# RWKV pairs: the layer norm of a pair's y is spread over the next pair's levels and scan, and the next pair's first products follow the last chunk directly

## The chip, the cores and the metric

The kernel runs on one core of a Trainium2 chip. The metric is the device time of one execution in microseconds (us), lower is better. Engines: PE (TensorE, matrix products), PEld (its weight loads), DVE (VectorE), ACT (ScalarE), POOL (GpSimd), SP (SyncE, which issues most loads).

## The reference, cut to what matters

The program is one block of mixed attention (NSA beside RWKV-7), followed by a second block; the change touches the RWKV part alone, which for S = 512 tokens and 8 heads of 64 computes

```
w = -softplus(-(w0 + tanh(wd) @ w_up)) - 0.5;  decay = exp(-exp(w))
a = sigmoid(a0 + ad @ a_up);  g = sigmoid(gd) @ g_up
kk = k * k_k, normed over each head;  kh = k * (1 + (a - 1) * k_a)
# scan over tokens, per head, state 64 x 64:
state = state * decay + (state @ -kk) (kk * a)^T + v kh^T;  y = state @ r
y = (y - mean) * rsqrt(var + eps) * ln_w + ln_b       # over each head
y = (y + sum(r * kh * r_k) * v) * g
```

## The kernel before, in words

All tensors lie with channels on the 128 partitions and the 512 tokens along the free axis, so a tile of 128 x 512 holds two heads, a *pair*. There are PAIRS = 4 pairs, one after the other. The scan over tokens is done in NCH = 8 chunks of 64.

A pair p goes through four parts:
- **The head** (function `head` on each engine): `w`, `a`, `g` are the low-rank products on PE, `sw`, `a`, `g` their copies on ACT. `kk0` scales the key, `kkq` squares it, `kss` sums over a head (PE, four products), `kstd` is the square root (ACT), `kmax`, `krec`, `krexp` (DVE) clip, invert and expand it, `krs` transposes it, `kkn` applies it. `cs`, `rel`, `dsum`, `relm` are the cumulative decays (DVE), `Ep`, `En`, `Em`, `D` their exponentials (ACT). `a1`, `kh`, `A`, `B`, `rk` (DVE) and `kka`, `K`, `R` (POOL) form the scaled operands, `bonus` the last term of y. `tokA`, `tokB`, `tokK`, `tokV` turn operands to token-major (PE, then ACT copies), `P1` and `P2` are the score products, taken out through a mask by DVE into TR and MR.
- **The levels**: a triangular inverse is built by doubling in five levels. In each, PE forms A (L2061), DVE takes it through a mask into Ap (`L1a`, `L1b`, ..., L1436), PE multiplies on both sides (X in L2070, Y in L2072) and ACT copies X and XT back. `XT0` (L1425) starts it, on an XT refilled with the identity (`eye`, L1408).
- **The scan**: after `MV`, `U0`, `WT`, each chunk c goes PE `u` (L2105), DVE `U` (L1449), PE `s` (L2115), DVE `S` (L1453), with `SD` (L1447) beside it. The output y gathers in PSUM bank 7 (L2091, L2098, L2119).
- **The norm of y**: ACT copies y (L863), PE takes the `mean`, DVE centres it (`yc`), ACT squares it (`ysq`), PE sums (`vss`), ACT takes the root (`vstd`, with its table of functions), DVE inverts and expands (`vrec`, `vrexp`), PE transposes (`vrs`), DVE forms `yn`, `yb`, `o`.

Each engine runs its instructions in the order of its program, and that order is written out by hand: the lists RW_PE_REST, RW_ACT_REST, RW_DVE_REST name the steps of pair p, and a step with "+" in front belongs to the head of pair p + 1, which is worked off between the levels of pair p. Each step raises its engine's semaphore by one, and the other engines wait for `upto(list, (name, pair))`. The names `given`, `done`, `took`, `made`, `own` in the code are such waits for PE, ACT, ACT, DVE and the own engine. All steps of a DVE head wait for the step before them on DVE itself. The eight PSUM banks are shared out by hand too: 0 and 1 serve the head and the norm, 2 and 3 the A products, 4 and 5 Y, 6 and 7 X.

Of the kernel before, what the change touches and what calls it, by code (L numbers as in the profile page):

```python
# [64 lines left out]
for _name, _n in [("ident", 128), ("means", 128), ("pair", 128), ("perm", 128)]:  # L65
# [5 lines left out]
RW_PE_HEAD = ["w", "a", "kss", "krs", "g", "bonus", "tokA", "tokB", "tokV", "P1a", "P1b", "tokK"]  # L71
RW_PE_REST = (["P2a", "+w", "+a", "P2b", "X0a", "X0b", "XSa", "XSb", "A1a", "A1b", "+kss", "X1a", "Y1a", "X1b", "Y1b",
               "A2a", "A2b", "+krs", "X2a", "Y2a", "X2b", "Y2b", "A3a", "A3b", "X3a", "Y3a", "X3b", "Y3b",
               "A4a", "A4b", "+g", "X4a", "Y4a", "X4b", "Y4b", "A5a", "A5b", "+bonus", "Y5a", "Y5b", "MV", "U0", "WT"]
              + [x for c in range(NCH) for x in ((f"u{c}", f"s{c}") if c < NCH - 1 else (f"u{c}",))]
              + ["y", "+tokA", "mean", "+tokB", "+tokV", "+P1a", "+P1b", "vss", "+tokK", "vrs"])
RW_ACT_HEAD = ["sw", "a", "kkq", "kstd", "Ep", "En", "Em", "D", "g", "tokA", "tokB", "tokV", "tokK"]
RW_ACT_REST = ["+sw", "+a", "+kkq", "X0a", "X0b", "X1a", "T1a", "X1b", "T1b", "+kstd", "X2a", "T2a", "X2b", "T2b",
               "+Ep", "+En", "X3a", "T3a", "X3b", "T3b", "+Em", "+D", "X4a", "T4a", "X4b", "T4b", "+g", "T5a", "T5b",
               "MV", "U0", "y", "+tokA", "+tokB", "+tokV", "ysq", "vstd", "+tokK"]  # L80
RW_DVE_HEAD = ["kk0", "cs", "rel", "dsum", "relm", "kmax", "krec", "krexp", "kkn", "a1", "kh", "A", "B",
               "rk", "bonus", "eye", "P1a", "P1b"]
RW_DVE_REST = (["XT0", "+kk0", "P2a", "P2b", "+cs", "+rel", "+dsum", "L1a", "L1b",
                "+relm", "+kmax", "+krec", "+krexp", "L2a", "L2b", "+kkn", "+a1", "+kh", "L3a", "L3b",
                "+A", "+B", "L4a", "L4b", "+rk", "L5a", "L5b", "+bonus", "WT"]
               + [x for c in range(NCH) for x in ((f"SD{c}", f"U{c}", f"S{c}") if c < NCH - 1 else (f"U{c}",))]
               + ["+eye", "yc", "+P1a", "+P1b", "vrec", "vrexp", "yn", "yb", "o"])


RW_POOL_HEAD = ["kka", "K", "R"]  # L90
RW_POOL_REST = ["+kka", "+K", "+R"]


def pair_steps(head, rest):

    steps = [(x, 0) for x in head]
    for p in range(PAIRS):
        steps += [(x[1:], p + 1) if x[0] == "+" else (x, p) for x in rest if x[0] != "+" or p + 1 < PAIRS]
    return steps


RW_PE, RW_ACT, RW_DVE = (pair_steps(RW_PE_HEAD, RW_PE_REST), pair_steps(RW_ACT_HEAD, RW_ACT_REST),
                         pair_steps(RW_DVE_HEAD, RW_DVE_REST))
# [44 lines left out]
def build(nc, A, out, first_block=True, second_block=True):  # L148
# [3 lines left out]
    with ExitStack() as ctx:  # L152
# [130 lines left out]
        if first_block:  # L283
# [3 lines left out]
            def mixer_phase(*tensors):  # L287
# [20 lines left out]
             eye, mask8) = mixer_phase(  # L308
# [6 lines left out]
                ("kst", [P, TT, 2], F32), ("krec", [P, TT, 2], F32), ("eye", [P, HD], F32),  # L315
# [8 lines left out]
            rmask = norm_t[:, 1]  # L324
            stri = mask8[:, 0:2 * HD]
# [159 lines left out]
        def _(pool):  # L485
# [90 lines left out]
        def _(act):  # L576
# [104 lines left out]
            if first_block:  # L681
# [118 lines left out]
                def head(p, *names):  # L800
# [4 lines left out]
                    for name in names:  # L805
# [31 lines left out]

                head(0, *RW_ACT_HEAD)

                AHEAD = {1: ("kstd",), 2: ("Ep", "En"), 3: ("Em", "D"), 4: ("g",), 5: ()}  # L840
                for p in range(PAIRS):
                    head(p + 1, "sw", "a", "kkq")

# [4 lines left out]
                    for n in range(2):  # L848
                        taken("X0" + "ab"[n], X, 6, n)
                    for lev in range(1, 6):  # L850
# [4 lines left out]
                        head(p + 1, *AHEAD[lev])  # L855
                    given(p, "MV")
                    rw(p, "MV", act.activation(MV, psum[:, 0, :], ACT.Copy))
                    given(p, "U0")
                    rw(p, "U0", act.activation(U0[:].rearrange("p c d -> p (c d)"), psum[:, 1, :],
                                               ACT.Copy))  # L860
                    given(p, "y")
                    act.wait_ge(rw_pool, upto(RW_POOL, ("K", min(p + 1, PAIRS - 1))))
                    rw(p, "y", act.activation(tA[:], psum[:, 7, :], ACT.Copy))  # L863
                    head(p + 1, "tokA", "tokB", "tokV")
                    done(p, "yc")
                    rw(p, "ysq", act.activation(tB[:], tC[:], ACT.Square))
                    given(p, "vss")
                    rw(p, "vstd", act.activation(kst[:].rearrange("p t c -> p (t c)"), psum[:, 1, 0:8], ACT.Sqrt,
                                                 bias=eps[:, 1:2], scale=1.0 / HD))
                    head(p + 1, "tokK")  # L870
# [121 lines left out]
        def _(dve):  # L992
# [167 lines left out]
            if first_block:  # L1160
# [184 lines left out]
                def head(p, *names):  # L1345
# [11 lines left out]
                    for name in names:  # L1357
                        if name == "kk0":
                            if p >= 2:
                                own(p - 2, "o")  # L1360
                            step("kk0", dve.tensor_scalar(tC[:], k, v("k_k", p), None, ALU.mult))
# [11 lines left out]
                        if name == "relm":  # L1373
                            given(p, "kss")
# [29 lines left out]
                        if name == "bonus":  # L1404
                            given(p, "bonus")
                            step("bonus", dve.tensor_tensor(tD, val, psum[:, 1, :], ALU.mult))
                        if name == "eye":
                            rw(p, "eye", dve.tensor_copy(XT[:], eye[:].unsqueeze(1).to_broadcast([P, 8, HD])))  # L1408
                        if name[0:2] == "P1":
                            keep_lower(p, name, TR, {"a": 3, "b": 4}[name[2]])  # L1410

                head(0, *RW_DVE_HEAD)

                AHEAD = {1: ("relm", "kmax", "krec", "krexp"), 2: ("kkn", "a1", "kh"), 3: ("A", "kka", "B", "K"),
                         4: ("R", "rk"), 5: ("bonus",)}
                for p in range(PAIRS):
                    D_p = Dc[:, p % 2]

                    def step(name, ins, wait=True):
                        rw(p, name, ins)  # L1420
                        if wait:
                            own(p, name)

                    own(p, "P1b")
                    step("XT0", dve.copy_predicated(XT[:], lmask[:, 0].unsqueeze(1).to_broadcast([P, 8, HD]), TR[:, :, 0]),  # L1425
                         wait=False)
                    head(p + 1, "kk0")
                    for name, b in (("P2a", 5), ("P2b", 2)):
                        keep_lower(p, name, MR, b)
                    head(p + 1, "cs", "rel", "dsum")  # L1430

                    for lev in range(1, 6):
                        mask = lmask[:, lev].unsqueeze(1).to_broadcast([P, 4, HD])
                        for n in range(2):
# [3 lines left out]
                                psum[:, 2 + n, 0:4 * HD].rearrange("p (m n) -> p m n", m=4)), wait=False)  # L1438
                        head(p + 1, *AHEAD[lev])
                    given(p, "WT")  # L1440
                    step("WT", dve.tensor_copy(WT[:], psum[:, 2, :]), wait=False)
                    done(p, "U0")
                    for c in range(NCH):
                        if c < NCH - 1:
                            if c >= 1:
                                own(p, f"S{c - 1}")
                            step(f"SD{c}", dve.tensor_scalar(SD[:], Sh[:, c], D_p[:, c:c + 1], None, ALU.mult), wait=False)  # L1447
                        given(p, f"u{c}")
                        step(f"U{c}", dve.tensor_tensor(Ut[:, c], U0[:, c], psum[:, 3, 0:HD], ALU.add), wait=False)  # L1449
                        if c < NCH - 1:  # L1450
# [950 lines left out]
```

## Time and profile before

| | us |
|---|---|
| median of 3 runs (lowest, highest) | 3045.91 (3044.82, 3048.0) |
| profiled execution | 3043.87 |
| its span, first to last instruction | 3042.2 |
| RWKV pairs within the span | from about 387 to 616 |
| PE busy over the span | 2893.9 (95%) |
| DVE, ACT, POOL busy | 1469.2, 973.6, 196.8 |
| mean granted clock of TensorE | 0.957 of 2.4 GHz |

The profile is of one execution. Times in its views count from the span's first instruction. In the timeline an instruction group "xN" is N instructions in a row, and a bracket tells how long its engine sat idle before it and who ended that; in the chain of waits each piece is what held up the end at that time, so that the pieces of a stretch add up to it.

### The profile page before, as it was taken

How to read it: one execution, taken by the hardware profiler on the slowest of the kernel's cores; microseconds unless marked ns; L12 is line 12 of the kernel's file. 1: busy time of each engine (PE TensorE's matmuls, PEld its weight loads, DVE VectorE, ACT ScalarE, POOL GpSimd, SP SyncE). 2: the span in 40 equal slices, each digit the busy share in tenths (PEclk: the TensorE clock that was granted, in tenths of full speed). 3: DMA queues.
4: the chain of work that ended last, by engine and by line, in shares of the span. 5: the costliest groups of instructions: out<-in, count | busy, mean ns of one | idle time of the engine just before them, and what ended most of it. 6: DMA issues, size and time to landing. Idle time of an engine off the chain costs nothing.

```text
span 3042.2 us, 39851 instructions
## 1 busy us (share of the span) xinstructions
PE 2893.9 (95%) x15739; PEld 2296.4 (75%) x15739; DVE 1469.2 (48%) x2135; ACT 973.6 (32%) x1540; POOL 196.8 (6%) x241
## 2 busy tenths in 40 slices
PE   7988978899999999999979999999999989999998
PEld 6844857778788787888858888788887753788887
DVE  4255655366677655555453332333323468433322
ACT  3334234333333223222233222322223236332222
POOL 1000010001200011000110000100001000100000
PEclk8669988999999999999979999999999999899999
DMA  6100500057322364555412223222232210122232
GB/s 225 59 1 1 187 16 2 3 187 235 131 96 97 100 201 157 193 192 190 154 53 90 96 94 92 84 104 97 94 94 96 83 63 1 56 87 96 94 93 72
DMA packets 89905, 309.17 MB, mean 102 GB/s; under 512 B 10288, under 2 KB 14000, under 8 KB 89648
## 3 DMA queue, kind: packets, MB, share of 16 engines
q1 hardware_dynamic: 69040, 231.84, 22.7%
q0 software_dynamic: 20736, 75.51, 7.4%
q8 instruction: 94, 1.54, 0.2%
q14 instruction: 35, 0.29, 0.0%
HBM read 305.21 MB, written 2.10 MB: 101 GB/s over the span
## 4 chain that ended last, share of the span: by engine, by line
PE 88%; DVE 7%; ACT 2%; issue 1%; DMA 0%; POOL 0%; SPq 0%; DVEq 0%; ACTq 0%
PE psum L1688 24%; PE psum L1690 24%; PE psum L1689 24%; PE psum L1912 1%; PE psum L1900 1%; PE psum L1852 1%; PE psum L1762 1%; PE psum L1702 1%; PE psum L1758 1%; DVE nmax L1623 1%; PE psum L1759 1%; PE psum L2017 1%; PE psum L2072 1%; PE psum L2237 1%; PE psum L1924 1%
## 5 line engine op out<-in xcount | busy, mean ns | idle before, releaser
L1000 DVE TENSOR_TENSOR w_lo<-stage,w_hi 128x1024 fp32r<-128x1024 f32 (+3 forms) x445 | 519.4, 1167 | 846.9 <-ACT w_hi L586 844.7
L1688 PE MATMUL psum<-h_hi,w_hi 128*128 128x512 f32 x2248 | 887.5, 395 | 12.2 <-POOL h_lo L566 8.3
L1689 PE MATMUL psum<-h_lo,w_hi 128*128 128x512 f32 x2248 | 879.0, 391 | 0.0
L1690 PE MATMUL psum<-h_hi,w_lo 128*128 128x512 f32 x2248 | 878.8, 391 | 0.0
L586 ACT ACTIVATE w_hi<-stage 128x1024 fp32r<-128x1024 f32 (+3 forms) x445 | 450.2, 1012 | 1281.1 <-PE psum L1690 1249.9
L1688 PEld LDWEIGHTS psum<-h_hi,w_hi 128*128 128x128 f32 x2248 | 423.8, 189 | 107.8 <-POOL h_lo L566 9.2
L1689 PEld LDWEIGHTS psum<-h_lo,w_hi 128*128 128x128 f32 x2248 | 423.9, 189 | 91.2 <-issue 3.4
L1690 PEld LDWEIGHTS psum<-h_hi,w_lo 128*128 128x128 f32 x2248 | 423.7, 188 | 89.9
L1688 PE MATMUL psum<-hid_hi,w_hi 128*128 128x512 f32 x880 | 342.9, 390 | 6.5 <-DVE hid L1085 6.5
L1689 PE MATMUL psum<-hid_lo,w_hi 128*128 128x512 f32 x880 | 342.4, 389 | 0.0
L1690 PE MATMUL psum<-hid_hi,w_lo 128*128 128x512 f32 x880 | 342.4, 389 | 0.0
L1688 PEld LDWEIGHTS psum<-hid_hi,w_hi 128*128 128x128 f32 x880 | 165.2, 188 | 42.9 <-DVE hid L1085 8.6
L1690 PEld LDWEIGHTS psum<-hid_hi,w_lo 128*128 128x128 f32 x880 | 165.2, 188 | 34.5
L1689 PEld LDWEIGHTS psum<-hid_lo,w_hi 128*128 128x128 f32 x880 | 165.2, 188 | 34.0
L1085 DVE TENSOR_TENSOR hid<-s_buf,psum 128x512 f32<-128x512 f32 x88 | 60.5, 687 | 266.9 <-PE psum L1690 265.2
L1036 DVE CUSTOM_DVE_ANT_0 mod_w<-mod_w,c_act 128x1024 f32<-128x1024 f32 x144 | 175.4, 1218 | 0.0
L494 POOL DMA_DIRECT2D mod_w<-in_mod_w x144 | 76.9, 534 | 1143.2 <-DVE modv L1036 965.9
L643 ACT ACTIVATE hid_hi<-hid 128x512 f32 (+1 forms) x110 | 68.0, 619 | 54.8 <-DVE hid L1085 54.8
L597 ACT ACTIVATE norm_t<-xT 128x512 f32<-128x512 f32 x64 | 40.3, 630 | 128.9 <-DVE xT L1109 121.6
L515 POOL TENSOR_TENSOR rexp<-norm_t 128x512 f32<-128x512 f32 x7 | 9.0, 1287 | 1086.4 <-ACT norm_t L597 1086.4
L1092 DVE TENSOR_TENSOR hid_lo<-hid,hid_hi 128x512 f32 (+1 forms) x110 | 75.2, 684 | 0.0
L515 POOL TENSOR_TENSOR rexp<-rexp,norm_t 128x512 f32<-128x512 f32 x35 | 45.1, 1288 | 268.4 <-ACT norm_t L597 268.4
(383 smaller groups left out, 2740.3 us busy)
## 6 DMA issues: line engine op xcount, KB each, us to landing
stage<-in_up SPq DMA_DIRECT2D x220, 512.0 KB, 3.2
mod_w<-in_mod_w POOLq DMA_DIRECT2D x144, 512.0 KB, 4.0
stage<-in_down SPq DMA_DIRECT2D x80, 448.0 KB, 3.3
stage<-in_down SPq DMA_DIRECT2D x40, 512.0 KB, 3.5
stage<-in_w_in SPq DMA_DIRECT2D x24, 512.0 KB, 3.3
stage<-in_w_qkv SPq DMA_DIRECT2D x24, 512.0 KB, 3.2
stage<-in_w_merge SPq DMA_DIRECT2D x16, 512.0 KB, 4.4
PTn<-in_cmp_w SPq DMA_DIRECT2D x1, 4096.0 KB, 12.1
```

Source lines behind the costliest of these rows:

```text
L494: pool.dma_start(mod_w[:, slot], A["mod_w"][bass.ds(t, 1)].rearrange("a p n -> (a p) n")).then_inc(mod_in[slot], 16)
L515: pool.tensor_tensor(sq_sum, sq(n_norm, 0) if k == 1 else sq_sum, sq(n_norm, k), ALU.add).then_inc(acc_done, 1)
L586: act.activation(w_hi[:, c % 2, 0:kt * cols], stage[:, c % NSTAGE, 0:kt * cols], ACT.Copy).then_inc(hi_done, 1)
L597: act.activation(sq(n_norm, k), xT[:, k], ACT.Square).then_inc(sq_done, 1)
L643: act.activation(hid_hi[:, bass.ds(2 * i + q, 1), :].rearrange("p a n -> p (a n)"), hid[:, q], ACT.Copy).then_inc(hidhi_done, 1)
L1000: dve.tensor_tensor(w_lo[:, c % 2, 0:kt * cols], stage[:, c % NSTAGE, 0:kt * cols], w_hi[:, c % 2, 0:kt * cols].bitcast(F32), ALU.subtract ...
L1036: dve.tensor_tensor_reduce(out=mod_w[:, t % 2], in0=mod_w[:, t % 2], in1=c_act[:], scale=1.0, scalar=0.0, op0=ALU.mult, op1=ALU.add, accum ...
L1085: dve.tensor_tensor(hid[:, q], s_buf[:, q], taps[:, 1] if f == 0 else bank(s.tile + 2 * q + 1), ALU.mult).then_inc(hid_done, 1)
L1092: dve.tensor_tensor(hid_lo[:, tile, :].rearrange("p a n -> p (a n)"), hid[:, q], hid_hi[:, tile, :].rearrange("p a n -> p (a n)").bitcast( ...
L1688: pe.matmul(dst, wh[:, n], a_hi[:, k], start=start and n == 0, stop=False)
L1689: pe.matmul(dst, wh[:, n], a_lo[:, k], start=False, stop=False)
L1690: m = pe.matmul(dst, wl[:, n], a_hi[:, k], start=False, stop=stop and n == kt - 1)
```

## The change

- The norm of pair p - 1 ("-" in the lists) is worked off in pair p: `yc` between P2a and P2b, `ysq` before level 1, `vss`, `vstd`, `vrec`, `vrexp` in level 4, `vrs` and `yn` after level 5, `yb` and `o` in the first two chunks of the scan. After the last pair it runs as before, on its own.
- After a pair's last chunk PE runs tokA, tokV, P1, P2a, tokB, `mean` and `bonus` of what follows; `tokK` moves behind level 1's A products.
- The head of pair p + 1 moves to later levels: `w` in 2, `a` in 3, `kss` in 4, `krs` after 5, `g` behind the y products that stand before the scan. On DVE, kk0 is in level 1, cs to relm in 3, kmax to krexp in 4, kkn, a1, kh, (yn), A, B, rk after 5 and ahead of the copy of WT. On ACT, sw, then a and kkq, then kstd, vstd, Ep, En, then Em, D.
- `eye` goes from DVE to POOL, between `kka` and `K`, where it waits for the pair's `WT` products.
- The norm gets its own buffers (yA, yC in zraw; vst, vrec); MV and U0 use banks 6 and 4; the bonus is written over r in zm.

```diff
+RW_PE_HEAD = ["w", "a", "kss", "krs", "g", "bonus", "tokA", "tokV", "P1a", "P1b", "P2a", "tokB"]
+RW_PE_REST = (["P2b", "X0a", "X0b", "XSa", "XSb", "A1a", "A1b", "tokK", "X1a", "Y1a", "X1b", "Y1b",
+               "A2a", "A2b", "+w", "X2a", "Y2a", "X2b", "Y2b", "A3a", "A3b", "+a", "X3a", "Y3a", "X3b", "Y3b",
+               "A4a", "A4b", "+kss", "-vss", "X4a", "Y4a", "X4b", "Y4b", "A5a", "A5b", "Y5a", "Y5b", "+krs", "-vrs",
+               "MV", "U0", "WT", "+g"]
...
+              + ["y", "+tokA", "+tokV", "+P1a", "+P1b", "+P2a", "+tokB", "mean", "+bonus"])
+RW_ACT_REST = ["X0a", "X0b", "-ysq", "X1a", "T1a", "X1b", "T1b", "tokK", "X2a", "T2a", "X2b", "T2b", "+sw",
+               "X3a", "T3a", "X3b", "T3b", "+a", "+kkq", "X4a", "T4a", "X4b", "T4b", "+kstd", "-vstd", "+Ep", "+En",
+               "T5a", "T5b", "+Em", "+D", "MV", "U0", "+g", "y", "+tokA", "+tokV", "+tokB"]
+RW_DVE_REST = (["XT0", "P2a", "-yc", "P2b", "bonus", "L1a", "L1b", "+kk0", "L2a", "L2b", "L3a", "L3b", "+cs", "+rel", "+dsum",
+                "+relm", "L4a", "L4b", "+kmax", "+krec", "+krexp", "-vrec", "-vrexp", "L5a", "L5b", "+kkn", "+a1", "+kh",
+                "-yn", "+A", "+B", "+rk", "WT", "SD0", "U0", "-yb", "S0", "SD1", "U1", "-o", "S1"]
...
+               + ["+P1a", "+P1b"])
+RW_POOL_HEAD = ["eye", "kka", "K", "R"]
+RW_POOL_REST = ["+kka", "+eye", "+K", "+R"]
...
+            yA, yC = zraw[:, 0, 0:S], zraw[:, 1, 0:S]
...
+            def refill_eye(p):
+
+                if p == 0:
+                    pool.wait_ge(zset, 8)
+                else:
+                    pool.wait_ge(rw_pe, upto(RW_PE, ("WT", p - 1)))
+                rw(p, "eye", pool.tensor_copy(XT[:], eye[:].unsqueeze(1).to_broadcast([P, 8, HD])))
...
+                            dve.wait_ge(rw_pool, upto(RW_POOL, ("R", p)))
+                            rw(p, "bonus", dve.tensor_tensor(r, val, psum[:, 1, :], ALU.mult))
```

## Rows read from the trace of the kernel before

**Rows 1.** Windows (start:end, length, busy of PE, PEld, DVE, ACT, POOL, clock, DMA).

```profile
519.50:574.10 54.60, 48.16 (x1004) 40.74 (x1000) 27.09 (x62) 20.16 (x41) 4.45 (x3) 0.87 0.01 2
530.00:532.00 2.00, 2.00 (x36) 1.80 (x36) 1.90 (x4) 0.38 (x1) 0.86 (x1) 0.50 0.00 0
554.00:556.00 2.00, 1.84 (x28) 1.38 (x24) 0.96 (x4) 0.00 (x0) 0.00 (x0) 0.50 0.00 0
```

**Rows 2.** Chain of waits (start, length, what), where parts of a pair begin or end.

```profile
441.45 0.28 PE psum L2105 x4
...
550.13 0.28 PE psum L2105 x4
...
562.61 1.66 PE psum L2017 x32
...
577.45 0.45 DVE Ap L1436
...
589.82 0.45 DVE Ap L1436
...
595.18 0.93 PE psum L2091 x32
...
607.09 0.61 ACT tA L863
```

**Rows 3.** Chain of waits, from the end of pair 1's scan to pair 2's levels.

```profile
507.97 1.67 PE psum L2017 x32
...
510.70 2.01 PE psum L2017 x64
512.71 1.75 PE psum L1963 x32
514.46 0.98 PE psum L2128 x8
...
517.26 0.76 DVE tC L1467
...
524.00 0.45 DVE Ap L1436
```

**Rows 4.** Timeline of ACT and of DVE, level 1 of pair 2.

```profile
527.02 1.28 ACT L820 ACT_TABLE_LOAD   x1
...
528.60 0.17 DVE L1378 TENSOR_SCALAR kst<-kst 128x8 f32<-128x8 f32 x1 [3.25 <-ACT kst L820]
...
529.50 0.77 DVE L1436 COPY_PREDICATED Ap<-mask,psum 128x256 f32<-128x256 uint8 x2
```

**Rows 5.** Chain of waits, head of pair 0.

```profile
400.43 2.09 PE psum L1998 x2
...
403.35 4.69 PE psum L2017 x96
...
412.66 1.02 PE psum L1963 x16
413.68 0.93 PE psum L2048 x32
```

**Rows 6.** Timeline, pair 0: rk beside POOL's K, and the first mask.

```profile
398.52 1.85 DVE L1402 SCALAR_TENSOR_TENSOR tB<-zm,vec,tA 128x512 f32<-128x512 f32 x1
398.56 1.26 POOL L540 TENSOR_TENSOR Kt<-Kt,tA 128x512 f32<-128x512 f32 x1 [2.08 <-DVE Bt L1400]
...
416.54 0.77 DVE L1436 COPY_PREDICATED Ap<-mask,psum 128x256 f32<-128x256 uint8 x2
```

**Rows 7.** Timeline of DVE, pair 2: kh, A, the copy of WT, S0.

```profile
531.55 1.64 DVE L1391 SCALAR_TENSOR_TENSOR tA<-tA,zm 128x512 f32<-128x512 f32 x1
...
538.39 0.69 DVE L1395 SCALAR_TENSOR_TENSOR stage<-tC,stage 128x512 f32<-128x512 f32 x1 [3.25 <-ACT stage L829]
...
549.31 0.69 DVE L1441 COPY WT<-psum 128x512 f32<-128x512 f32 x1 [4.18 <-PE psum L2089]
...
551.17 0.28 DVE L1453 SCALAR_TENSOR_TENSOR Sh<-psum,Dc,SD 128x64 f32<-128x64 f32 x1 [0.51 <-PE psum L2115]
```

More of the change, by code:

```diff
@@ L68 @@
 NCST = _at
[L71 to L74, printed above, removed]
-              + [x for c in range(NCH) for x in ((f"u{c}", f"s{c}") if c < NCH - 1 else (f"u{c}",))]
-              + ["y", "+tokA", "mean", "+tokB", "+tokV", "+P1a", "+P1b", "vss", "+tokK", "vrs"])
@@ L77 @@
[L77 to L91, printed above, removed]
@@ new lines @@
+RW_ACT_HEAD = ["sw", "a", "kkq", "kstd", "Ep", "En", "Em", "D", "g", "tokA", "tokV", "tokB"]
+RW_ACT_REST = ["X0a", "X0b", "-ysq", "X1a", "T1a", "X1b", "T1b", "tokK", "X2a", "T2a", "X2b", "T2b", "+sw",
+               "X3a", "T3a", "X3b", "T3b", "+a", "+kkq", "X4a", "T4a", "X4b", "T4b", "+kstd", "-vstd", "+Ep", "+En",
+               "T5a", "T5b", "+Em", "+D", "MV", "U0", "+g", "y", "+tokA", "+tokV", "+tokB"]
+RW_DVE_HEAD = ["kk0", "cs", "rel", "dsum", "relm", "kmax", "krec", "krexp", "kkn", "a1", "kh", "A", "B", "rk", "P1a", "P1b"]
@@ L104 @@
+RW_PE = pair_steps(RW_PE_HEAD, RW_PE_REST, ("vss", "vrs"))
+RW_ACT = pair_steps(RW_ACT_HEAD, RW_ACT_REST, ("ysq", "vstd"))
+RW_DVE = pair_steps(RW_DVE_HEAD, RW_DVE_REST, ("yc", "vrec", "vrexp", "yn", "yb", "o"))
 RW_POOL = pair_steps(RW_POOL_HEAD, RW_POOL_REST)
@@ L1412, in _, with step @@
                 head(0, *RW_DVE_HEAD)
-                AHEAD = {1: ("relm", "kmax", "krec", "krexp"), 2: ("kkn", "a1", "kh"), 3: ("A", "kka", "B", "K"),
-                         4: ("R", "rk"), 5: ("bonus",)}
+                AHEAD = {1: ("kk0",), 3: ("cs", "rel", "dsum", "relm"), 4: ("kmax", "krec", "krexp"), 5: ("kkn", "a1", "kh")}
                 for p in range(PAIRS):
                     D_p = Dc[:, p % 2]
-                    def step(name, ins, wait=True):
+                    def step(name, ins):
@@ L1420, in step @@
                         rw(p, name, ins)
-                        if wait:
-                            own(p, name)
                     own(p, "P1b")
[L1425 to L1430, printed above, removed]
+                    dve.wait_ge(rw_pool, upto(RW_POOL, ("eye", p)))
@@ L1432, in _ @@
+                    step("XT0", dve.copy_predicated(XT[:], lmask[:, 0].unsqueeze(1).to_broadcast([P, 8, HD]), TR[:, :, 0]))
+                    keep_lower(p, "P2a", MR, 5)
+                    spread_of_y(p - 1, "yc")
+                    keep_lower(p, "P2b", MR, 2)
+                    head(p, "bonus")
                     for lev in range(1, 6):
@@ L2039, in _ @@
                     more = p + 1 < PAIRS
-                    scores(p, "P2a", Kt, 5)
-                    head(p + 1, "w", "a")
-                    took(p, "tokV")
-                    scores(p, "P2b", Kt, 2)
+                    head(p, "P2b")
                     took(p, "tokA")
@@ L2121, in _ @@
                     rw(p, "y", last)
-                    head(p + 1, "tokA")
+                    head(p + 1, "tokA", "tokV", "P1a", "P1b", "P2a", "tokB")
                     took(p, "y")
-                    rw(p, "mean", pe.matmul(psum[:, 0, :], pair_ones, tA[:], start=True, stop=True))
-                    head(p + 1, "tokB", "tokV", "P1a", "P1b")
-                    took(p, "ysq")
-                    for t in range(TT):
-                        last = pe.matmul(psum[:, 1, 2 * t:2 * t + 2], tB[:, t * P:(t + 1) * P], head_of, start=True, stop=True)
-                    rw(p, "vss", last)
-                    head(p + 1, "tokK")
-                    made(p, "vrexp")
-                    for t in range(TT):
-                        last = pe.transpose(psum[:, 1, t * P:(t + 1) * P], MV[:, t * P:(t + 1) * P], ident)
-                    rw(p, "vrs", last)
+                    took(*((p + 1, "g") if more else (p, "tokK")))
+                    rw(p, "mean", pe.matmul(psum[:, 0, :], pair_ones, yA, start=True, stop=True))
+                    head(p + 1, "bonus")
+                spread_of_y(PAIRS - 1, "vss", "vrs")
                 pe.wait_ge(rw_dve, upto(RW_DVE, ("yn", PAIRS - 1)))
```

211 lines of the change are left out of this document (132 added, 79 removed).

## The prediction

> **What bounds the kernel now.** Over the whole span TensorE carries the chain, and the change touches only the RWKV stage, so I looked at the granted clock and busy time by stretch there, then the chain of waits for the milestones of a pair, then each engine's timeline. One pair period with a next pair beside it is 54.6 us, TensorE busy 48.2 of it at a mean clock of 0.87 [rows 1]. It falls to half (1.2 GHz) twice: behind the pause in level 1, and from about the fourth chunk of the scan [rows 1].
>
> A pair has three parts. Call L the start of the first level mask (DVE L1436), u the first chunk product (L2105), e the scan's end. In pair 2, L = 524.00, u = 550.13, e = 562.61, and L of pair 3 is 577.45 [rows 2, 3]. So levels 26.1, scan 12.5, tail 14.8 (16.0 after pairs 0 and 1: 507.97 to 524.00 [rows 3]). Pair 3, with no next pair, shows the bare levels: four in 12.37 us (577.45 to 589.82), L to u 18.7, and its scan, at full clock, takes 11.0 (to 607.09) [rows 2]. Against pair 2's 12.5 that makes a half-clock chunk 0.3 dearer. Pair 0's levels end at 441.45, 24.9 after L at 416.54 [rows 2, 6].
>
> The tail is a row of PE products: tokA 1.67 at half clock, mean 1.06, tokB with tokV 2.0, P1 1.75, vss 0.98, tokK and vrs, until DVE takes over at 517.26 with yn, yb, o, kk0, P2, cs, rel, dsum before the mask at 524.00 [rows 3]. In the levels the large hole is the key norm: ACT loads the square-root table at 527.02, DVE can start kmax at 528.60 and only at 529.50 the next mask, because the masks are queued behind kmax, krec, krexp [rows 4]. A bare mask would start at about 527.1 (0.5 behind the last product of the level, which ends 0.4 before the load).
>
> **The change, part by part.**
>
> *Head.* tokA no longer waits for DVE's bonus (402.52 to 403.35), and tokK, w and a leave the stretch before L. From the end of the bonus product at 402.52 [rows 5]: tokA and tokV at half clock 3.3 (three took 4.69), P1 2.0 (1.75, part slow), P2a and P2b 1.9 (1.02 for one), tokB 1.0, X0 0.93 and XS as much, A1's half, on which the mask waits, 0.5 (estimated). That is 10.5, L = 413.0 instead of 416.54: **-3.5**. DVE's two P1 masks, XT0, P2 and bonus fit beside it.
>
> *Tail.* After e: tokA 1.67, tokV 0.95, P1 1.75, P2a 0.9, tokB 0.95, mean 1.06, bonus 1.06, P2b 1.0, X0 and XS 1.8, half of A1 0.5 = 11.6. DVE's chain is now short: P2b's copy and bonus end about 0.8 before L. So 16.0 + 16.0 + 14.8 becomes 3 x 11.6: **-12.1**.
>
> *Levels.* The work is not gone; it comes back here. In a middle pair (1 or 2), from L: four bare levels 12.4, plus tokK 1.0, w and a 1.05, kss and vss 0.98 each [rows 3], less 1.1 because these products fill PE's short waits for a mask (estimated 0.27 a level). One wait is new: kss needs ACT's kkq, queued behind T3b and the sigmoid a, three ACT steps of some 0.6, ready 1.7 behind the level's last product, while A4a and A4b cover 0.95: 0.7. Together 16.0. Then the hole of [rows 4] in level 4: the masks L5a, L5b are queued behind kmax, krec, krexp, as L2a, L2b were, and now behind vrec and vrexp too (0.20 and 0.43, the sizes of krec and krexp, with their gaps 0.7). L2a came 2.4 late; L5a comes 3.1 late, at 19.1. Y5a follows at 19.6.
>
> What follows Y5a before u was 5.8 in pair 3 (590.3 to 596.1) [rows 2]. Now DVE has kkn, a1, kh, yn, A, B, rk in its queue *before* the WT copy, for which PE and u wait. krs is there 1.85 behind Y5a (Y5 1.1, four transposes 0.7); then kkn 0.72, a1 0.52, kh 1.67 [rows 7], yn 0.78, A 0.73 [rows 7], B 0.73. rk has a bound on each side: 0.75 for such a step alone, 1.85 beside POOL's K, which starts with it as here [rows 6]. I take 1.85. WT's copy 0.7 [rows 7]. That is 9.6, and 0.1 to the first chunk product. PE's own work to there (Y5, krs, vrs, MV, U0, WT, the y products, g) is about 8.0 and hidden.
>
> The refill of XT ("eye") moves from DVE (0.42, in the shadow of the scan) to POOL, between kka and K, where it waits for WT's products, 6.1 behind Y5a. R and K are queued behind it; P1 of the next pair waits for R, but the scan of 12 us covers that. No row shows a POOL copy. Its time lies between DVE's 0.42 and POOL's two-input 1.26 [rows 6]; I take 0.8. It runs when A and B want to. The row shows that DVE steps with two SBUF inputs stand still beside a POOL step: rk 1.85 beside K, kh 1.64 beside kka, but the equal-sized A 0.69 alone [rows 6, 7]. Whether a one-input copy blocks too is open: nothing or 0.8; I take 0.8, as all POOL steps seen block. So u = 19.6 + 10.5 = 30.1, instead of 26.1: +4.0 in each of pairs 1 and 2. [...]
>
> Pair 0 has no vss, vrec, vrexp, yn: 30.1 - 1.0 - 0.7 - 0.8 = 27.6 against 24.9: +2.7. Pair 3 adds tokK 1.0, vss 1.0, vrs 0.6 and the hole: vstd still needs the table load before vrec, vrexp and L5: 2.2. That is +4.8. Sum of the levels: **+15.5**.
>
> *Scan.* yb (0.75) sits between U0 and S0, o (0.69) between U1 and S1. DVE has been idle 0.51 there [rows 7], so each costs 0.3, in three pairs 1.8. SD0 may meet POOL's R: nothing to 0.7; I take 0.2 each. **+2.4**.
>
> *Clock.* PE now pauses 3.2 us in level 4 and up to 2.4 before u, and scans at the same density as now. In [rows 1] a 2-us pause and the sparse scan were followed by 0.50. In pairs 0 to 2 the longer DVE queue hides a slow PE before u; in pair 3 nothing does (1.5). Slow chunks so far: 3, 5, 5 and 0; all 32 slow would be 19 x 0.3 = 5.7 more. I take **+2.5** in all, bounds -8.4 (below) and +7.2.
>
> *Unmoved.* ACT goes from four table loads a pair to three, but the one that hurts stays on the chain. POOL's later modulation loads issue some 8 us later, with some 60 us of cover; SP's load behind the last o follows the stage end. The last pair's norm from e to yn keeps its 8 us with nothing beside it.
>
> Sum: -3.5 - 12.1 + 15.5 + 2.4 + 2.5 = +4.8. The profiled execution took 3043.87 (span 3042.2 and 1.7 around it), 2.0 under the median of the runs, so 3048.7 in a profile and **3050.7** as median. 0.2% is 6.1 us, which is also about what a measurement here can tell from no change.
>
> **Rivals.** *The tail's gain shows and the clock holds.* Half clock now costs 8.4: level 2 of pairs 1 and 2 (estimated 1.2 each), 13 chunks (3.8), three tokA (1.67 against 0.95: 2.2). If the denser products after e and the shorter levels 1 to 3 keep 2.4 GHz throughout, the sum is 4.8 - 2.5 - 8.4 = -6.1: 3039.8. For it: pair 3 ran its whole scan at full clock after dense levels. Against: the pause in level 4 is longer than the one after which the clock fell. It decides only if next to no scan chunk is slow, or if the two blocks by POOL are missing too. Chance 0.12.
>
> *The levels become the bound by more than the tail gives, at half clock.* All scans slow and pair 3's products too: 7.2 instead of 2.5, 3055.4. For it: the pause stands 10 us ahead of every scan. It crosses 0.2% from 3.8 of clock cost on, or if the hole and the queue before WT are 0.5 dearer in each pair. Chance 0.30.
>
> *Hardly anything moves:* PE has as much work, the holes change place, the blocks on DVE are half as dear and the clock as before: about 3045. Chance 0.20. The forecast itself (3046.5 to 3052.0) has 0.38. Within 0.2%: 0.58; slower 0.30; faster 0.12. The range takes the low bounds of the blocks with part of the clock gain (3040) and the slow rival with its margin (3057).
>
> **What the profile would show.** From e to the next L 11.6 without the DVE chain; in level 4 kst, krec, vrec and an expansion ahead of L5, PE idle about 3 us; the WT copy behind rk with rk near 1.85 and POOL's copy in between; u 30 behind L; U0 and S0 0.3 farther apart. L to u under 28 would mean that I have the DVE queue before WT wrong; a tail over 13 that DVE still binds it; a granted clock near 1.0 in the scans is the fast rival.

## The result: the changed kernel is 0.3% slower, and the profile after

| | before | after |
|---|---|---|
| median (lowest, highest; 9 runs each) | 3046.84 (3044.82, 3050.72) | 3055.09 (3051.19, 3061.77) |
| ratio, 95% interval | | 1.0031 [1.0023, 1.0040] |
| profiled execution, its span | 3043.87, 3042.2 | 3059.8, 3058.0 |
| mean granted clock | 0.957 | 0.951 |

The time lies in the range (3040 to 3057), on the slow side: it is the time of the rival with more half clock (3055.4), not that of the forecast (3050.7). The changed kernel was profiled once more (f4), which gives a second sample of each part. "Stage" is the time from VectorE's copy of the identity, ahead of pair 0, to the first product behind the RWKV part; the head ends at the first L (the first level mask of a pair), u is the first chunk product, and a tail runs from the end of a scan to the next L. Of all executions below one, of f1, was slow (3674.69 at a mean clock of 0.737); it is in f1's median and not in its ratio.

| us | before | predicted | after | after, again |
|---|---|---|---|---|
| head of pair 0 | 29.1 | 25.6 | 25.6 | 24.4 |
| L to u, pairs 0 to 3 | 24.8, 26.1, 26.1, 18.5 | 27.6, 30.1, 30.1, 23.5 | 29.5, 32.8, 32.9, 25.6 | 28.5, 32.8, 32.9, 25.7 |
| scans, sum | 48.3 | 50.7 | 50.5 | 50.3 |
| tails | 16.0, 16.0, 14.8 | 11.6 each | 12.2, 12.2, 12.0 | 11.7, 11.8, 11.8 |
| end of the stage | 8.5 | 8.5 | 9.2 | 8.5 |
| clock, not shared out | | +2.5 | (in the parts) | (in the parts) |
| stage | 228.2 | 233.0 | 242.5 | 238.5 |

The predicted parts add up to 233.4; the forecast was 228.2 + 4.8 = 233.0, and the 0.4 is rounding and its two starting values (24.9 and 18.7, read from the chain of waits, where this table has 24.8 and 18.5 from the timeline).

The medians differ by 8.3, the stages of single profiles by 14.3 and 10.3. Most of that gap lies in which executions were profiled: before's was 3.0 under its median, the changed kernel's 4.7 over its own (3059.8), so the two are 15.9 apart, and f4's (3054.53) is 10.7 over before's. Outside the stage single profiles differ as well: among the profiles of this study, whose code is the same up to there, the stage begins at 385.3 to 391.8 us. So a part is read from its own stretch, and a total from the ratio to the kernel before.

First the granted clock. Windows of the changed kernel (start:end, length, busy of PE, PEld, DVE, ACT, POOL, clock, DMA): the stage from pair 0's first mask, the period from pair 1's L to pair 2's, and three stretches in it.

```profile
412.51:629.38 216.87, 185.79 (x3739) 157.78 (x3735) 96.29 (x215) 73.31 (x148) 14.09 (x12) 0.82 0.01 2
...
465.96:524.09 58.13, 50.80 (x1001) 43.25 (x998) 28.10 (x60) 20.69 (x41) 4.76 (x4) 0.82 0.01 2
481.00:484.00 3.00, 3.00 (x64) 3.00 (x60) 0.00 (x0) 1.15 (x3) 0.00 (x0) 0.50 0.00 0
...
488.00:494.00 6.00, 5.69 (x72) 5.13 (x72) 3.15 (x5) 2.29 (x6) 1.51 (x1) 0.50 0.00 0
505.00:512.00 7.00, 6.45 (x87) 4.95 (x86) 2.78 (x11) 0.01 (x1) 0.00 (x0) 0.50 0.01 2
```

The period was 54.6 us at 0.87 [rows 1]; it is 58.1 at 0.82. The whole stretch of the first line stood at 0.90 before (416.54 to 615.60). Half clock stands in the scan as before, and now, in pairs 1 and 2, at two places of the levels: in pair 1 from 481, and from 488. The chain of waits says what the engine did around them (pair 1's levels, with the tail ahead; start, length, what).

```profile
453.72 3.41 PE psum L2072 x64
457.14 2.64 PE psum L2021 x48
...
460.71 1.06 PE psum L2193 x2
...
470.15 1.12 PE psum L2034 x2
...
474.21 1.05 PE psum L2038 x2
...
478.29 0.53 ACT norm_t L846
...
478.86 1.05 PE psum L2045 x8
...
480.81 0.90 PE psum L2144 x16
...
484.71 1.28 ACT L849
486.00 0.19 ACT kst L849
486.21 0.18 DVE kst L1415
...
486.65 0.44 DVE norm_t L1419
...
487.35 0.44 DVE zraw L1468
487.81 0.45 DVE Ap L1502
```

The tail is TensorE's alone, as predicted: where [rows 3] had VectorE's chain, products follow one another (L2072 and L2021 are tokens and scores, L2193 the mean). The hole is that of [rows 4], moved to level 4 and two steps longer. w (L2034) and a (L2038) stand 4 us apart, 1.12 and 1.05. kss and vss (L2045, L2088) follow a wait for ACT's square, and behind them the X product (L2144), 0.47 elsewhere, takes 0.90: the clock has fallen before the hole. In the hole are the steps that were named, from the table load over kst, kmax, krec, krexp, vrec and vrexp to the mask (L1502). Ahead of all this, pair 0 reaches its first mask 4.0 us earlier than in [rows 6], at 412.51, 3.5 of it in the head.

What VectorE, GpSimd and TensorE did ahead of u, in the timeline of the changed kernel, pair 1:

```profile
496.52 0.75 DVE L1439 SCALAR_TENSOR_TENSOR tB<-zm,vec,tA 128x512 f32<-128x512 f32 x1
497.31 0.69 DVE L1511 COPY WT<-psum 128x512 f32<-128x512 f32 x1
497.92 1.10 DVE L1517 TENSOR_SCALAR SD<-Sh,Dc 128x64 f32<-128x64 f32 x1
...
499.29 1.44 DVE L1475 SCALAR_TENSOR_TENSOR zraw<-zraw,vec,zm 128x512 f32<-128x512 f32 x1
...
496.93 0.81 POOL L552 COPY XT<-eye 128x512 f32<-128x512 f32 x1 [3.23 <-PE psum L2156]
497.71 1.26 POOL L558 TENSOR_TENSOR Kt<-Kt,tA 128x512 f32<-128x512 f32 x1
498.93 1.26 POOL L560 TENSOR_TENSOR AR<-AR,zm 128x512 f32<-128x512 f32 x1
...
488.31 1.97 PE L2146 MATMUL psum<-XT,Ap 64*64 64x64 f32 x32 [3.01 <-DVE Ap L1502]
...
497.72 1.12 PE L2041 MATMUL psum<-zm,g_up 128*128 128x512 f32 x2
498.78 0.33 PE L2173 MATMUL psum<-Sh,WT 64*64 64x64 f32 x4
```

The last line is u, 32.8 behind L, where [rows 2, 3] have 26.1 in pair 2. Y5 (L2146) waited 3.01 for the mask and ran at half clock. WT's copy is out at 498.00, but u starts at 498.78: TensorE, at half clock from 488 to 494, had only then finished g. Before, WT's copy was the last thing ahead of u, with VectorE idle until then [rows 7]. rk took 0.75, not the 1.85 of [rows 6]: this time the identity's copy stood beside it, had started behind it and took 0.81 itself, and K started only after rk.

### The profile page after: what moved, and what is told of

Its sections match the earlier page's. It is cut to its first block, busy times and chain, and to the rows that moved or that the text cites. A ratio compares the mean times of both kernels' runs of the same rounds, so it can differ in the third digit from the quotient of the medians.

```text
span 3058.0 us, 39859 instructions
## 1 busy us (share of the span) xinstructions
PE 2908.0 (95%) x15739; PEld 2310.0 (76%) x15739; DVE 1471.6 (48%) x2131; ACT 971.4 (32%) x1538; POOL 198.1 (6%) x245
## 4 chain that ended last, share of the span: by engine, by line
PE 89%; DVE 7%; ACT 2%; issue 1%; POOL 0%; DMA 0%; SPq 0%; DVEq 0%; ACTq 0%
PE psum L1746 24%; PE psum L1747 24%; PE psum L1748 24%; PE psum L1970 1%; PE psum L1958 1%; PE psum L1910 1%; PE psum L1760 1%; PE psum L2146 1%; PE psum L1820 1%; DVE nmax L1681 1%; PE psum L2072 1%; PE psum L1816 1%; PE psum L1817 1%; PE psum L2144 1%; PE psum L2298 1%
## 5 line engine op out<-in xcount | busy, mean ns | idle before, releaser
L1746 PE MATMUL psum<-h_hi,w_hi 128*128 128x512 f32 x2248 | 888.6, 395 | 12.2 <-POOL h_lo L593 8.3
## 6 DMA issues: line engine op xcount, KB each, us to landing
PTn<-in_cmp_w SPq DMA_DIRECT2D x1, 4096.0 KB, 12.2
```

The source lines that it names most:

```text
L1746: pe.matmul(dst, wh[:, n], a_hi[:, k], start=start and n == 0, stop=False)
```

## The experiments

Each starts from the changed kernel unless it says otherwise; the code shown is shortened, with lists written out. The ratios are to the kernel before, run on the same chip. Where the intervals of two ratios overlap, their difference is not clear of noise.

**e1: the masks of level 5 first.**

```diff
-"L4a", "L4b", "+kmax", "+krec", "+krexp", "-vrec", "-vrexp", "L5a", "L5b", "+kkn"
+"L4a", "L4b", "L5a", "L5b", "+kmax", "+krec", "+krexp", "-vrec", "-vrexp", "+kkn"
```

> Edit to the changed kernel: DVE takes the level-5 masks before kmax, krec, krexp, vrec, vrexp instead of behind them. Theory H (the hole in level 4, masks queued behind the square roots, is the dearest new cost): the 3.1 us between the last product of level 4 and Y5 go to 0.5, krs moves up by some 2, L to u falls from 33 to 28 to 30 in the middle pairs and by 2.2 in pair 3; the stage gets 9 to 12 us shorter, the run comes back to before or a little under it (3042 to 3048). Rival Q (the DVE steps before the copy of WT bound u, whenever the masks come): the hole moves behind Y5, where krs waits for krexp, and L to u falls by under 1.5 a pair. Rival C (half clock from level 4 on is the cost, and it has its own cause ahead of the hole): the stretch from X4 to MV stays at 1.2 GHz, and only half of the 3 us comes back.

3046.73 (10 runs), ratio 0.9999 [0.9989, 1.0008]: the whole loss is gone. L to u is 26.2, 28.9, 28.9, 21.5, 2.3 to 4.2 less in each pair; the scans of this profile are 2.1 longer in sum than in the first one of the changed kernel (52.6). Timeline of e1, pair 1:

```profile
479.74 1.28 ACT L849 ACT_TABLE_LOAD   x1
479.89 0.91 DVE L1502 COPY_PREDICATED Ap<-mask,psum 128x256 f32<-128x256 uint8 x2 [5.44 <-PE psum L2132]
...
480.39 1.15 PE L2146 MATMUL psum<-XT,Ap 64*64 64x64 f32 x32
...
482.17 0.66 PE L2052 MATMUL psum<-cst,norm_t 128*128 128x128 f32 x4 [0.64 <-DVE norm_t L1419]
...
488.62 1.12 PE L2041 MATMUL psum<-zm,g_up 128*128 128x512 f32 x2
489.11 0.69 DVE L1511 COPY WT<-psum 128x512 f32<-128x512 f32 x1
```

Y5 runs beside the table load, and of the hole only a wait of krs is left, 0.64. Y5 starts 19.4 behind L instead of 22.3, and u follows 9.5 behind it instead of 10.5, as these products now run at full clock. Now g ends (489.74) and WT's copy ends (489.80) together, so the queue ahead of WT is a bound of the same size. The clock still falls behind kss and vss.

**e2: w and a behind one another in the queue again.**

```diff
-"A2a", "A2b", "+w", "X2a", ..., "A3a", "A3b", "+a", "X3a"
+"A2a", "A2b", "+w", "+a", "X2a", ..., "A3a", "A3b", "X3a"
```

> Edit to the changed kernel: the products w and a stand together in level 2 as they did before, instead of w in level 2 and a in level 3. Theory W (the two use one half of the array's rows each and ran beside each other before, 1.05 for both; apart they take 1.12 and 1.05): levels 2 and 3 together get 1.1 us shorter in each of three pairs, 3.3 in all, 0.1% of the run. Rival: they take 2.1 together too, and nothing moves; the mis-sized term of my sum is then something else.

3053.21 (10 runs), ratio 1.0021 [1.0011, 1.0031], 0.0010 below the changed kernel's ratio, which is 3.0 us; the two intervals overlap. TensorE in the timeline of e2:

```profile
468.49 0.69 PE L2034 MATMUL psum<-zm,low_up 64*128 64x512 f32 x1
468.50 0.69 PE L2038 MATMUL psum<-zm,low_up 64*128 64x512 f32 x1
...
469.03 0.59 PE L2038 MATMUL psum<-zm,low_up 64*128 64x512 f32 x1
```

Both products use half of the array's rows (64*128), w one half and a the other. Next to each other, as in the kernel before, they run at the same time, 1.1 us for both from 468.49 to 469.62; apart, each takes 1.05 to 1.12 on its own. My 1.05 for both was the duration of two that overlap. In this profile the level-5 mask starts 0.7, 1.6 and 1.0 earlier behind L in pairs 0 to 2 than in the first one of the changed kernel, and at the same place in pair 3, which has neither product. L to u is 27.7, 30.2, 32.7, 25.7.

**e3: products without a use that keep TensorE busy**, one of 512 columns ahead of kss, three in the hole of level 5 (their results are read by nobody).

```diff
+                        if lev == 4 and more:
+                            took(p + 1, "sw")
+                            filler(1)    # pe.matmul(psum[:, 0, :], ident, cst[:, 0:512], ...)
...
+                        if lev == 5:
+                            filler(3)
```

> Edit to the changed kernel: PE gets products without a use, one of 512 columns ahead of kss in level 4 and three behind A5b, in the hole; nothing else moves, and no result changes. Theory C (the low activity in level 4, the wait for kkq, the two-column products kss and vss and the hole, brings half clock, which then lasts to MV and comes early in the scan): the granted clock stays at 1.0 through level 4 to u, X4/Y4 take 1.9 instead of 3.4, Y5 to MV 3.3 instead of 5.9; L to u falls from 33 to about 30 in pairs 1 and 2, where DVE's queue then binds, pair 3 by 3; 5 to 9 us in all. Rival H (only the hole's length counts, the clock would have been hidden behind DVE): under 2 us.

3053.28 (10 runs), ratio 1.0022 [1.0012, 1.0031]; L to u 27.6, 31.0, 31.0, 23.4. A window over pair 1's levels in e3, then its timeline ahead of u:

```profile
467.30:498.30 31.00, 27.99 (x631) 22.58 (x625) 16.66 (x29) 16.43 (x33) 4.70 (x4) 1.00 0.01 3
```

```profile
494.47 0.61 POOL L552 COPY XT<-eye 128x512 f32<-128x512 f32 x1 [2.01 <-PE psum L2165]
494.56 1.06 DVE L1437 TENSOR_TENSOR Bt<-Bt,Kt 128x512 f32<-128x512 f32 x1
...
495.66 1.86 DVE L1439 SCALAR_TENSOR_TENSOR tB<-zm,vec,tA 128x512 f32<-128x512 f32 x1
495.70 1.26 POOL L558 TENSOR_TENSOR Kt<-Kt,tA 128x512 f32<-128x512 f32 x1 [0.63 <-DVE Bt L1437]
...
497.55 0.69 DVE L1511 COPY WT<-psum 128x512 f32<-128x512 f32 x1
...
498.30 0.33 PE L2182 MATMUL psum<-Sh,WT 64*64 64x64 f32 x4 [1.92 <-DVE WT L1511]
```

With the clock at 1.0 the levels are what the prediction drew, VectorE's queue ending last and rk 1.86, and in pairs 1 and 2 0.9 longer, which w and a apart explain. Half clock costs the levels 119.9 or 120.8 (two profiles) less 113.0: 7 to 8 us. By the ratios only 2.7 us of it is there (1.0031 less 1.0022), and their intervals overlap. In this profile the scans are 1.4 longer, and what lies outside the stage is 2.0 and 3.5 longer than in the two profiles of the changed kernel. So 7 to 8 us is what single profiles show of the levels, and the run's gain is less.

**e4: WT's copy right behind kh; yn, A, B, rk, yb, o one by one in the scan.**

```diff
-"+kh", "-yn", "+A", "+B", "+rk", "WT", "SD0", "U0", "-yb", "S0", "SD1", "U1", "-o", "S1"
+"+kh", "WT", "SD0", "U0", "-yn", "S0", "SD1", "U1", "+A", "S1", "SD2", "U2", "+B", "S2",
+"SD3", "U3", "+rk", "S3", "SD4", "U4", "-yb", "S4", "SD5", "U5", "-o", "S5", ...
```

> Edit to the changed kernel: the copy of WT comes right behind kh on DVE; yn, A, B, rk, yb, o follow one each behind U0 to U5 of the scan. Theory Q of my prediction (DVE's seven steps before the copy of WT set u): u comes 2 to 3 us earlier in pairs 0 to 2, each moved step costs 0 to 0.3 in the scan, 4 to 7 us in all. Rival C (in the profile of the changed kernel PE, at half clock, ends g 0.8 after the copy of WT, so PE sets u): L to u stays within 0.3 us of 33, and the whole moves by under 2 us, of which 0.8 a pair comes from SD0 and yb no longer standing beside POOL's K and R.

3064.19 (4 runs), ratio 1.0055 [1.0038, 1.0072]. L to u is 28.2, 31.6, 32.9, 24.3, at most 1.3 less than in the changed kernel, because TensorE at half clock sets u in pairs 0 to 2. The scans are 14.2, 14.6, 14.4, 12.9. Timeline of e4, fourth chunk of pair 1:

```profile
506.80 1.04 DVE L1515 TENSOR_SCALAR SD<-Sh,Dc 128x64 f32<-128x64 f32 x1
...
507.89 1.67 DVE L1439 SCALAR_TENSOR_TENSOR tB<-zm,vec,tA 128x512 f32<-128x512 f32 x1
...
506.53 1.26 POOL L558 TENSOR_TENSOR Kt<-Kt,tA 128x512 f32<-128x512 f32 x1 [5.93 <-DVE Bt L1437]
507.75 1.27 POOL L560 TENSOR_TENSOR AR<-AR,zm 128x512 f32<-128x512 f32 x1
```

SD, 0.25 alone, takes 1.04 beside K, and rk 1.67 beside R: in the scan, where VectorE is in every round trip, such a meeting is paid: this chunk took 3.12 us, the one before it 1.58.

**g1: the identity's copy back on VectorE behind the scan**, GpSimd keeping kka, K, R.

```diff
-RW_POOL_REST = ["+kka", "+eye", "+K", "+R"]
+RW_POOL_REST = ["+kka", "+K", "+R"]      # and "+eye" ahead of "+P1a" in RW_DVE_REST
```

> The changed kernel with one part undone: the copy of the identity is again on VectorE behind the scan, and GpSimd keeps kka, K and R. Lock theory (a GpSimd copy from SBUF to SBUF holds up VectorE's steps beside it): B falls from 1.06 to about 0.5 in each pair, K then starts right behind B and stands beside rk, which becomes about 1.85, and R beside what follows; SD0 goes from 1.10 back to 0.25 where R no longer meets it. VectorE pays about 0.3 us for the copy itself behind the scan, hidden behind the wait for TensorE. Net 0 to -1 us a pair, 3052 to 3056 in all, against 3055 for the changed kernel. Rival (the lock is by chance, it only follows whatever VectorE does at that time): B, rk and SD0 together cost the same, nothing moves by over 0.2 us a pair.

3055.24 (10 runs), ratio 1.0029 [1.0019, 1.0038]: no change. The 3052 to 3056 that the theory named hold this too, so the time decides nothing between it and the rival. Timeline of g1, pair 1:

```profile
491.94 1.85 DVE L1437 SCALAR_TENSOR_TENSOR tB<-zm,vec,tA 128x512 f32<-128x512 f32 x1
...
494.44 0.54 DVE L1520 TENSOR_SCALAR SD<-Sh,Dc 128x64 f32<-128x64 f32 x1
...
495.09 0.74 DVE L1475 SCALAR_TENSOR_TENSOR zraw<-zraw,vec,zm 128x512 f32<-128x512 f32 x1
...
491.98 1.27 POOL L558 TENSOR_TENSOR Kt<-Kt,tA 128x512 f32<-128x512 f32 x1 [2.86 <-DVE Bt L1435]
493.20 1.72 POOL L560 TENSOR_TENSOR AR<-AR,zm 128x512 f32<-128x512 f32 x1
```

The durations moved as the lock theory said for rk (0.75 to 1.85) and yb (1.44 to 0.74); SD0 fell to 0.54, not to 0.25, and B had no 0.37 to give in this pair (0.69 in both). The sum of the four is 3.98 in the changed kernel and 3.82 here. So the block is real, and having the copy on GpSimd is not what the change costs; what all blocks together cost this run does not show, since K and R still hold up what stands beside them.

**f1, f2, f3: from e1 on.** f1 has the masks first and w and a together. f2 moves yb and o to the chunks after U3 and U4, away from K and R. f3 adds to f2 e3's one product without a use ahead of kss.

```diff
-"WT", "SD0", "U0", "-yb", "S0", "SD1", "U1", "-o", "S1"
+"WT", "SD0", "U0", "S0", ..., "SD3", "U3", "-yb", "S3", "SD4", "U4", "-o", "S4"
```

> Both edits of the first two experiments on the changed kernel: the level-5 masks ahead of kmax to vrexp, and w and a together in level 2. Theory: the two gains lie in different levels and add up, so the stage is 1.05 shorter in each of three pairs than with the masks alone, 229.0 to about 226, and the run 3 us under it: 3043.5, a little under the kernel before. Rival: what w and a give back is lost again, because cs, rel, dsum, relm on DVE then bind level 4: 3046 to 3047.

> As the run with both edits, and yb and o move from behind U0 and U1 to behind U3 and U4. Theory P (yb took 1.4 to 1.6 instead of 0.75 because POOL's R or K held it up, which cost 0.8 to 1.1 in the first chunk of pairs 1 and 2): the first chunk period falls from 2.5 to 1.5 to 1.9 (SD0 may still stand beside K), yb is back at 0.75, the stage gets 1 to 2 us shorter. Rival: K and R now hold up something else in the scan and the sum stays.

> As the run before, and PE gets one 512-column product without a use in level 4 ahead of kss, where it waits 0.7 to 0.9 for kkq. Theory C: this and not the long hole set the early fall of the clock in pairs 1 and 2 (with the masks first it still fell at the level-4 products), so X4 and Y4 run at 2.4 GHz, 1.9 instead of 3.4: 1 to 1.5 less in each of pairs 1 and 2, up to 3 us less in the run. Rival: the clock falls at the same place or a few us later all the same, and the product costs 0.2 a pair.

f1: 3043.73 (10 runs), ratio 0.9988 [0.9977, 0.9999]. f2: 3041.56 (12 runs), 0.9982 [0.9974, 0.9991]; in pair 1 its first chunk's period is 1.45 where the changed kernel's is 2.26 (1.6 in f4). f3: 3040.19 (11 runs), 0.9974 [0.9966, 0.9983]. L to u in f3 is 25.5, 26.7, 26.7, 21.5. Neighbours in this row overlap in their intervals; f3 against e1 does not. Windows of f3, pair 1's levels and its scan:

```profile
464.27:490.93 26.66, 24.53 (x624) 21.22 (x618) 15.53 (x29) 15.65 (x33) 3.52 (x3) 1.00 0.01 3
490.93:503.53 12.60, 10.61 (x157) 8.10 (x158) 6.93 (x24) 0.60 (x1) 1.57 (x2) 0.67 0.01 1
```

One product ahead of kss is enough for these levels: pair 1's stand at 0.94 in f2, which lacks only this product, and take 28.1 instead of 26.7. In the scan the clock still falls.

**f4: the changed kernel again.** 

> The changed kernel once more, to see how much of a single profile's stage time repeats: the scheduled parts (head 25.6, tails 12, the hole 3.1) should repeat within 0.2; the stretches at half clock may lie elsewhere, and L to u and the scan differ by up to 1.5 us a pair.

One run, 3054.53. Its parts stand in the table of the result: the levels repeat within 0.1 in three pairs and 1.0 in pair 0, the scan of pair 3 differs by 1.0 and the tails by 0.2 to 0.5.

**g2, h2: short products without a use in the scan of f3**, g2 with two of 64 columns in each chunk, h2 with the first only.

```diff
                         rw(p, f"u{c}", last)
+                        pe.matmul(psum[:, 1, 0:HD], ident, cst[:, 0:HD], start=True, stop=True)
                         if c < NCH - 1:
...
                                              stop=c == NCH - 1, skip_group_check=True)
+                        if c < NCH - 1:     # g2 only
+                            pe.matmul(psum[:, 1, 0:HD], ident, cst[:, 0:HD], start=True, stop=True)
```

> f3 (masks first, w and a together, y's and o's copies later, one product without a use ahead of kss) with one 64-column product without a use behind u's product and one behind y's part in every chunk of the scan. Theory (TensorE's clock falls in the scans for its short waits between products, as it did in the levels ahead of kss): the clock stays at 1.0 in the scans and each takes 11.5 us instead of 12.0 to 12.7, so 3036 to 3039 against 3040.2 for f3. Rival (the scan's waits are on VectorE's round trip, and the clock falls all the same): each product adds up to 0.1 us at half clock on TensorE's way, 16 of them in a pair, and the scans take 12.5 to 14 us: 3041 to 3045.

> g2 with only one of the two 64-column products in each chunk, the one behind u's. Theory (one is enough to hold the clock, and the other stood between y's part and the next u, where it cost about 0.1 us a chunk): clock 1.0 in the scans, scans 11.5 us instead of 12.3, stage 210 us, 3031 to 3033. Rival (one is too little, the clock falls as in f3): scans about 12.5 to 13, stage 218 to 220, 3039 to 3042.

g2: 3034.77 (5 runs), ratio 0.9966 [0.9951, 0.9980]. h2: 3031.28 (4 runs), 0.9944 [0.9927, 0.9960], the fastest kernel here. Scans 12.3 each in g2 and 11.8 to 11.9 in h2, tails 10.7 in both. The stages are 213.3 and 212.5; the rest of the difference of their medians is not in the stage, and the intervals overlap. Windows of h2, the stage from pair 0's first mask, and pair 1's scan:

```profile
415.21:603.31 188.10, 169.03 (x3809) 143.89 (x3805) 94.76 (x215) 71.12 (x148) 14.99 (x12) 0.99 0.01 3
489.85:501.76 11.91, 10.23 (x174) 8.19 (x176) 6.92 (x24) 0.60 (x1) 1.57 (x2) 1.00 0.01 1
```

Against f3 the scan of pair 1 gives 0.7, and each tail 0.7 to 1.3, because tokA and what follows start at full clock. A chunk at full clock is 1.44 long without such products, 1.53 in h2 and 1.60 in g2: the first costs 0.09, the second, between y's part and the next u, 0.07.

**h1: the kernel before with g2's two products in the scan**, nothing else.

> The kernel before with nothing changed but the two 64-column products without a use in each chunk of the scan (behind u's product and behind y's part). In g2 they held the clock at 1.0 through all four scans and every tail was 10.7 us. If that gain belongs to the scan alone, it is there without the change too: clock 1.0 in the scans, scans 12.3 us each (12.0, 12.6, 12.6, 11.1 before), tokA at full clock (0.7 less a tail), the pause in level 1 still at half clock: the stage is 1 to 3 us shorter, 3044 to 3046 against 3046.8. Rival (the denser levels of g2 are what holds the clock, the scan's products alone do not): the clock falls in the scans as before, and the products cost 1 to 2 us a pair, 3048 to 3053.

3046.15 (10 runs), ratio 0.9991 [0.9982, 1.0001], not clear of no change; scans 12.3 each, tails 15.3, 15.3, 14.1, stage 226.0 instead of 228.2. The stage in one window of h1, from pair 0's first mask:

```profile
420.88:617.87 196.99, 177.77 (x3809) 151.82 (x3808) 91.34 (x214) 71.45 (x145) 13.36 (x9) 0.97 0.01 3
```

The clock holds in the scans without the change too. The scans' sum is 0.9 longer for the products, the tails are 2.1 shorter, and the levels of pair 2 1.6, as the clock doesn't fall in its level 1. With the clock held in the scans of both, g2's stage is 12.7 shorter than h1's, and by the ratios the run is 7.6 us shorter (0.9991 less 0.9966, with intervals that do not overlap): that is what spreading the norm is worth here once its own losses are mended, the product ahead of kss included.

## Why the prediction was right or wrong, point by point

The time came out 4.4 us over the forecast: 0.9 of it because before's median was 3045.91 when the forecast was made and 3046.84 beside the result, 3.5 because the change cost 8.3 and not 4.8. That it came so near is partly luck. In the profiles the stage was 9.5 and 5.5 us over the sum, most of it in the levels, where two terms were too small and two others too large.

**Head and tail: right.** -3.5 was -3.5 and -4.7 in the two profiles (the clock came back to full at 405.9 and at 403.8). The tails lost 3.8, 3.8 and 2.8, 10.4 in all (11.5 in the second profile) where 12.1 was taken. What is missing is tokV: I had tokA at half clock and tokV at full (2.62 together), and both ran at half clock (3.41).

**The hole in level 4: right, and it is the dearest of the new costs.** L5a was to come 3.1 late; Y5 waited 3.01 for it. e1 shows the price: 0.9999 against 1.0031, 9.8 us, as much as the whole loss. In pair 1 the products from Y5 to u gain 1.0 besides the 2.9 by which Y5 comes earlier, since behind the hole they had run at half clock.

**The term that failed first: "w and a 1.05".** Apart they take 2.17, 1.1 more in each of pairs 0 to 2, some 3.2 in all. e2 gives 3.0 back and f1 3.4 against e1, each with overlapping intervals; e2's masks of level 5, 3.2 earlier over three pairs, show it directly.

**The term that failed second: "I take +2.5" for the clock.** Its bounds held (-8.4, +7.2), but 5.4 to 6.3 was needed in the levels alone: they are 8.6 to 9.5 over the parts of the sum without it, 3.2 of that from w and a. The step behind it, "In pairs 0 to 2 the longer DVE queue hides a slow PE before u", failed in pairs 0 to 2 of the first profile, where TensorE reached u 1.1, 0.8 and 0.8 after the end of WT's copy (in f4 only in pair 2). I had 8.0 us of products behind Y5a from durations at full clock. It took 10.5 in pair 1: at half clock Y5 is 1.97, krs and vrs 1.9 together, MV 1.9, and only U0, WT, the y products and g ran at full clock again. I had also looked for the fall only behind the pause. In pairs 1 and 2 it came before, behind the wait for kkq and 2 us of two-column products which count as busy. With one 512-column product ahead of them the clock stood at 1.0 over the levels (f3; e3, with three more in the hole).

Where the time was lost tells the two apart. In pairs 1 and 2 the mask of level 5 started 21.9 behind L, where the sum had 19.1: w and a, and level 4 at half clock (with the clock held, in e3, it starts at 20.6). From that mask to u it took 11.0 in both, as in the sum. This agreement is luck: TensorE at half clock set u, and the queue of VectorE was shorter than taken (in pair 1 rk took 0.75 for 1.85, and B did not wait for the identity's copy).

**The queue ahead of WT: right where it binds.** With the clock at 1.0 (e3) it sets u, at 31.0 against 30.1 plus 1.05 for w and a. rk was 1.86 (taken 1.85). The identity's copy lengthened B by 0.37 (taken 0.8). The Trainium skill (SBUF — State Buffer, section "SBUF: two separate sides") has whichever of the two engines comes first hold the shared ports for its whole instruction, for VectorE steps with two SBUF inputs (against a GpSimd step that reads SBUF, as all of these do) or in a two-port mode. The traces agree both ways for the steps with two inputs: B waits for the copy in e3, and R takes 1.72 instead of 1.26 where it starts behind rk in g1. The one-input SD0 takes 1.10 beside K; by that rule it would have to run in a two-port mode, which no run here shows. WT's copy, which reads PSUM, keeps its 0.69 beside R in e3.

**The scan: right in sum, by luck, wrong in parts.** +2.4 was taken, +2.2 and +2.0 came. o cost nothing; yb cost 0.8 in pair 1, as R stood beside it (1.44 instead of 0.75), and 0.2 where R did not (f4, pair 1).

**The rivals.** The fast one did not occur by itself, and its premise was sound: with the clock held nearly throughout, g2 and h2 are 10 and 17 us below before by their ratios, though that took the masks, w and a, yb and added products too. The slow rival named the right kind of cost in the wrong place: scans as before, the levels slow.

What stays open: why the ratio of e3 gives back 2.7 us where its levels give 7 to 8 (its intervals, its longer scans and the time outside the stage leave room for much of it); and why h2's median is 3.5 below g2's where its stage is 0.8 shorter (with 4 and 5 runs the intervals allow both).

## What to carry to other kernels

Before spreading a chain over another's shadows, look at what its first step is queued ahead of: here a few small steps of VectorE ahead of a mask made a change that shortened the head by 3.5 and the tails by 10.4 us come out slower, and putting the mask first gave 9.8 back. Price moved products both at the clock they had and at half of it, and look for neighbours that ran side by side on the two halves of the array before separating them. If a stretch is at half clock with TensorE seemingly busy, one product without a use in front of its thinnest work is a cheap trial.

## What the runs showed of the hardware beyond that

- The granted clock fell to half behind a wait of 0.65 and sixteen two-column products during which PE counts as busy (the X product at 480.81 took 0.90 instead of 0.47), and did not with one 512-column product ahead of them (f3: 1.00 over pair 1's levels; f2, without it: 0.94).
- In the scan a single product of 64 columns per chunk held the clock at 1.00 for all of it (h2) and lengthened a chunk by 0.09, from 1.44 to 1.53; without it the window stands at 0.67 (f3), and the scan is 0.7 longer though it has less work.
- GpSimd's copy of 128x512 with one input took 0.61 where it came first (e3) and 0.81 where rk had started 0.41 before it, so the wait is also GpSimd's.
- A table load of ACT took 1.28, and the activation behind it started 0.01 after its end (484.71 and 486.00).
